# A decoder layer on one core: halved low parts of the keys, gate steps dealt by slot work, the down projection written token by token

## What is computed

```
a = rms_norm(h); projections of a: three mixers' q, k, v, and 3 x 1024 merge gates
A  sparse attention, 8 heads x 64: compressed keys (31 blocks), selected blocks, window of 256
B  differential attention, 4 heads: softmax(q1 k1) - lam softmax(q2 k2), values 128 wide, sub-norm
C  forgetting attention, 8 heads x 64, bias from a cumulated forget gate
merged = sum over mixers of sigmoid(gate) * (o @ w_br);  h = h + merged @ w_o
u, g = split(rms_norm(h) @ w_up);  h = h + (gelu(causal_conv3(u)) * g) @ w_down
```

## Time and profile before

| | us |
|---|---|
| median of 3 runs | 1049.41 |
| the profiled execution's own time | 1049.83 |
| its span in the trace | 1047.9 |
| TensorE busy | 1014.6 |
| VectorE busy | 576.9 |
| ScalarE busy | 413.0 |
| GpSimd busy | 80.8 |

### The profile page before, as it was taken

One profiled execution on the slowest core, in us unless ns is written; L12 is line 12 of the kernel. 1 busy time (PEld: TensorE's weight loads), 2 busy tenths in 40 slices (PEclk: granted clock), 3 DMA queues, 4 the chain that ended last, 5 costly groups with the idle time before them and its releaser, 6 DMA issues.

```text
span 1047.9 us, 13105 instructions
## 1 busy us (share of the span) xinstructions
PE 1014.6 (97%) x5133; PEld 850.4 (81%) x5133; DVE 576.9 (55%) x1056; ACT 413.0 (39%) x746; POOL 80.8 (8%) x66
## 2 busy tenths in 40 slices
PE   6899899999999999999899999999999999999998
PEld 5687789898887877888689888888888888888886
DVE  5645777773546678355655445465655656522123
ACT  4235445443446665424654433342322323221120
POOL 3200000000000000030000022011121111200000
PEclk9999899999999999999999999999999999999999
DMA  6512100102222211232211124222322323223222
GB/s 241 197 47 81 41 8 36 41 1 81 81 81 80 81 41 41 81 121 81 81 41 42 41 81 165 114 83 81 107 94 83 118 81 115 86 86 115 81 81 81
DMA packets 14653, 86.91 MB, mean 83 GB/s; under 512 B 1408, under 2 KB 3968, under 8 KB 5120
## 3 DMA queue, kind: packets, MB, share of 16 engines
q1 hardware_dynamic: 14592, 86.07, 23.1%
HBM read 83.96 MB, written 2.10 MB: 82 GB/s over the span
## 4 chain that ended last, share of the span: by engine, by line
PE 88%; DVE 7%; ACT 2%; issue 2%; DMA 1%; SPq 0%; DVEq 0%; ACTq 0%
PE ps L1280 20%; PE ps L1282 20%; PE ps L1281 20%; PE ps L1450 11%; PE ps L1436 5%; PE ps L1308 4%; PE ps L1422 2%; DVE k_ll L961 2%; PE ps L1423 2%; PE ps L1420 1%; DVE wl L855 1%; PE ps L1335 1%; PE ps L1413 1%; DVE nmx L1049 1%; DMA ident<-consts 1%
## 5 line engine op out<-in xcount | busy, mean ns | idle before, releaser
L855 DVE TENSOR_TENSOR wl<-raw,wh 128x512 fp32r<-128x512 f32 (+2 forms) x118 | 171.5, 1458 | 127.2 <-ACT wh L588 125.1
L588 ACT ACTIVATE wh<-raw 128x2048 fp32r<-128x2048 f32 (+1 forms) x58 | 109.4, 1886 | 155.9 <-PE ps L1282 138.3
L1280 PE MATMUL ps<-aT_h,wh 128*128 128x512 f32 (+1 forms) x376 | 146.7, 390 | 0.7 <-DVE aT_l L864 0.7
L1281 PE MATMUL ps<-aT_l,wh 128*128 128x512 f32 (+1 forms) x376 | 146.4, 389 | 0.0
L1282 PE MATMUL ps<-aT_h,wl 128*128 128x512 f32 (+1 forms) x376 | 146.4, 389 | 0.0
L737 ACT ACTIVATE prob<-ps,nmx 128x384 f32<-128x384 f32 (+3 forms) x128 | 66.7, 521 | 125.6 <-DVE nmx L1049 125.1
L1280 PE MATMUL ps<-wh,aT_h 128*128 128x512 f32 x256 | 102.4, 400 | 3.3 <-DVE smT L917 3.3
L1282 PE MATMUL ps<-wh,aT_l 128*128 128x512 f32 x256 | 101.1, 395 | 0.0
L1281 PE MATMUL ps<-wl,aT_h 128*128 128x512 f32 x256 | 100.9, 394 | 0.0
L1280 PEld LDWEIGHTS ps<-aT_h,wh 128*128 128x128 f32 (+1 forms) x376 | 70.0, 186 | 16.2 <-issue 0.9
L1282 PEld LDWEIGHTS ps<-aT_h,wl 128*128 128x128 f32 (+1 forms) x376 | 70.0, 186 | 15.3
(11 more groups left out here) (209 smaller groups left out, 1765.8 us busy)
## 6 DMA issues: line engine op xcount, KB each, us to landing
raw<-wblk SPq DMA_DIRECT2D x72, 1024.0 KB, 4.8
x<-x SPq DMA_DIRECT2D x4, 512.0 KB, 5.0
w_sb<-w SPq DMA_DIRECT2D x1, 2048.0 KB, 9.3
hid<-x SPq DMA_DIRECT2D x1, 2048.0 KB, 7.7
out<-outt SPq DMA_DIRECT2D x4, 512.0 KB, 3.1
stage<-consts SPq DMA_DIRECT2D x1, 1216.5 KB, 11.0
later<-consts SPq DMA_DIRECT2D x1, 448.0 KB, 12.0
par<-params SPq DMA_DIRECT2D x1, 204.5 KB, 7.8
```

The source lines that it names most:

```text
L588: nc.scalar.activation(wh[b % 2][:, 0:n], raw[b % RING][:, 0:n], ACT.Copy).then_inc(hi_ready, 4)
L855: ins = nc.vector.tensor_tensor(wl[b % RING][:, cols], raw[b % RING][:, cols], wh[b % 2][:, cols].bitcast(f32), ALU.subtract)
L1280: nc.tensor.matmul(dst, a_h, b_h, start=start, stop=False)
L1281: nc.tensor.matmul(dst, a_h, b_l, start=False, stop=False)
```

## The change

1. VectorE writes `k_ll` in DIFF and FOX in the head's own half only. GpSimd zeroes the other half once, after NSA's last scores, and TensorE waits for that (`k_zero`) ahead of DIFF's first unit. The product q_lo k_lo is left out.
2. ScalarE copies `small` to `smT`, ahead of its split of block `nq1`; VectorE no longer does.
3. NSA's first compressed scores, their norm, transposition and values stand ahead of unit 0, among 44 gate steps (40 before). The split of block `gate1` stands there too.
4. The other gate steps are dealt by an estimate of each slot's work (`slot_work`): the longer a slot keeps VectorE or ScalarE against TensorE, the more steps it gets. In DIFF most slots with an O get 0 to 2 and those with a C 5 to 13 (5 or 6 each before). In FOX slots get 9 falling to 1 (4 or 5 before). In NSA every second slot from 37 on gets none.
5. The down projection takes activations as the stationary operand and 512 weight columns as the moving one, so a bank holds 128 tokens by 512 output columns. `yT`, its copies and the 32 transposing matmuls go; VectorE adds bank and `hid` directly, and 8 DMAs of 256 KB send the result. `outt` lies at offset 0.

```diff
+def slot_work(m, events):
+    pe = dve = act = 0
+    for e in events:
+        if e[0] in ("S", "C", "A", "O"):
+            n = span(units_of(m)[e[1]])[1]
+        if e[0] == "S":
+            pe += 3 * (n * 2 // 5 + 20)
+            dve += n + 180
+            act += n * 4 // 5 + 420
+        elif e[0] == "C":
+            dve += 3 * n // 2 + 1000 if m == DIFF else 400
+        elif e[0] == "A":
+            pe += n * 5 // 6
+            if pv_index(m, e[1]) % 2:
+                act += n * 4 // 5 + 200
+            else:
+                dve += n + 150
+        elif e[0] == "O":
+            pe += n * 8 // 5
+            dve += 300
...
+    return pe, max(dve, act)
@@ attention_events
-        head += 8
-        put(-2, "SC", 0)
-        put(-1, "G", head, head + 8)
-        put(1, "CN", 0)
-        put(2, "TC", 0)
-        put(3, "OC", 0)
+        head += 20
...
-    for j in range(slots):
-        n = FILL - tail - head
-        put_fill(j, head + n * j // slots, head + n * (j + 1) // slots)
-        if j < U:
-            put(j, "S", j)
+    for j in range(U):
+        put(j, "S", j)
...
+    n = FILL - tail - head
+    work = [slot_work(m, at.get(j, [])) for j in range(slots)]
+    low, high = 0, 20000
+    while high - low > 1:
+        level = (low + high) // 2
+        if sum(max(0, max(level, 9 * o // 8) - p) for p, o in work) > n * 220:
+            high = level
+        else:
+            low = level
+    room = [max(0, max(high, 9 * o // 8) - p) for p, o in work]
+    done = 0
+    for j in range(slots):
+        f0 = head + n * done // sum(room)
+        done += room[j]
+        put_fill(j, f0, head + n * done // sum(room))
...
-        first += [("T", 0), ("G", HEAD_FILL[m], HEAD_FILL[m] + 8), ("T", 1)]
+        first = [("G", 0, 8), ("SC", 0), ("G", 8, 24), ("T", 0), ("CN", 0), ("G", 24, 32), ("T", 1), ("TC", 0), ("G", 32, 40), ("OC", 0), ("G", 40, head)]
+        for piece in range(4):
+            first[piece - 4:piece - 4] = [("W", BI[(m, "gate1")], piece), ("WL", BI[(m, "gate1")], piece)]
@@ scalar, NSA
                     split(BI[(m, "nq0")])
+                    full(act, ("P", m, "small", 0))
+                    b = place[("P", m, "small", 0)][0]
+                    nc.scalar.activation(smT[:, :], ps[b][0:32, :], ACT.Copy).then_inc(psum_free[b], 1)
                     split(BI[(m, "nq1")])
@@ vector
-                            lows = [k_ll[home, n, :], k_ll[other, n, :]]
+                            lows = [k_ll[home, n, :]]
...
             for d in range(KD):
-                if d % 2 == 1:
-                    full(dve, ("Y", d))
-                    b = place[("Y", d)][0]
-                    nc.vector.tensor_copy(yT[:, d, :], ps[b][:, :]).then_inc(psum_free[b], 1)
-                if d >= 2:
-                    finish(d - 2)
-            finish(KD - 2)
-            finish(KD - 1)
+                t, cols = d // 2, slice(d % 2 * S, d % 2 * S + S)
+                full(dve, ("Y", d))
+                nc.vector.tensor_tensor(outt[:, t, cols], bank(("Y", d))[:, :], hid[:, t, cols], ALU.add).then_inc(out_ready, 1)
@@ gpsimd
+            full(pool, ("S", NSA, len(units_of(NSA)) - 1))
+            nc.gpsimd.memset(k_ll[64:128, 0:8:2, :].bitcast(f32), 0.0)
+            nc.gpsimd.memset(k_ll[0:64, 1:8:2, :].bitcast(f32), 0.0).then_inc(k_zero, 1)
@@ tensor
+                            if m == DIFF:
+                                pe.wait_ge(k_zero, 1)
                         scores(j)
...
-                    cols = slice(d * P, (d + 1) * P)
+                    rows, cols = slice(d // 2 * P, d // 2 * P + P), slice(d % 2 * S, d % 2 * S + S)
                     for k in range(2):
-                        ins = passes(ps[d][:, :], h[:, k, cols], l[:, k, cols], acts[k][0], acts[k][1], first and k == 0, last and k == 1)
+                        f = 2 * n + k
+                        ins = passes(ps[d][:, :], actT_h[:, f, rows], actT_l[:, f, rows], h[:, k, cols], l[:, k, cols],
+                                     first and k == 0, last and k == 1)
                     if last:
                         done(("Y", d), ins)
-                        if d >= 2:
-                            finish(d - 2)
@@ sync
-            for n in range(4):
-                sp.wait_ge(out_ready, 2 * n + 2)
-                sp.dma_start(outv[:, :, n * 256:(n + 1) * 256], outt[:, :, n * 256:(n + 1) * 256]).then_inc(out_done, 16)
+            for d in range(KD):
+                t, cols = d // 2, slice(d % 2 * S, d % 2 * S + S)
+                sp.wait_ge(out_ready, d + 1)
+                sp.dma_start(outv[:, t, cols], outt[:, t, cols]).then_inc(out_done, 16)
```

More of the change, by code:

```diff
@@ L277, in build @@
         plan(("Y", d), d)
-    for d in range(KD):
-        plan(("YT", d), d)
     with ExitStack() as ctx:
@@ L832, in _ @@
                 split(B_DOWN + n)
-            for d in range(0, KD, 2):
-                full(act, ("Y", d))
-                b = place[("Y", d)][0]
-                nc.scalar.activation(yT[:, d, :], ps[b][:, :], ACT.Copy).then_inc(psum_free[b], 1)
         @block.vector
@@ L913, in post @@
                         ins.then_inc(cpe_ready, 1)
-                elif name == "small":
-                    full(dve, ("P", m, name, 0))
-                    b = place[("P", m, name, 0)][0]
-                    nc.vector.tensor_copy(smT[:, :], ps[b][0:32, :]).then_inc(psum_free[b], 1)
             def post_t(m, name, part=0):
@@ L1595, in _ @@
                         up_chunk(i, b, c)
-            def finish(d):
-                free(pe, ("Y", d))
-                transposes(("YT", d), [yT[:, d, t * P:(t + 1) * P] for t in range(TT)])
             def down(n):
@@ L1608, in down @@
                 h, l = [w[:, :].rearrange("p (k c) -> p k c", k=2) for w in (wh[blk % 2], wl[blk % RING])]
-                acts = [[t[:, 2 * n + k, :] for t in (actT_h, actT_l)] for k in range(2)]
                 for d in range(KD):
```

36 lines of the change are left out of this document (20 added, 16 removed).

## The result

| | before | change |
|---|---|---|
| median of 4 runs, us | 1049.38 (1049.29 to 1049.77) | 1042.7 (1041.7 to 1043.19) |
| the profiled execution's own time | 1049.83 | 1042.52 |
| its span | 1047.9 | 1040.7 |

The ratio is 0.9934, with a 95% interval of 0.9917 to 0.9952. So the change is faster, by 6.7 us where 24.3 were forecast. The time lies 10.7 us above the upper end of the range.

A forecast was written before the change was run, and what follows sets the result against it. The prediction took TensorE's own order, with its waits and half clock, to bound the kernel. Terms of -5.0, -5.6, -5.8, -2.3 and -5.6 sum to 24.3 us below the profiled 1049.83; with the median 0.4 lower, 1025.1 us, range 1021 to 1032.

The forecast's parts named there:

- Dealing the steps: Gate steps dealt by work: waits for `probT` in DIFF go, less new waits in slots without steps; -2.3 us.
- the 1.24 us: In DIFF, the time from a full transposition's start to the end of its copy, used to price slots without steps.
- The gain of 4.1 us: DIFF's four waits for VectorE's and two for ScalarE's `probT`, all expected to go under 8 to 13 steps.
- the dealing makes as many waits as it takes: Rival: DIFF gains nothing or loses, +4.9 instead of -2.3, NSA's thirteen stepless slots add 4; 1032 to 1036 us; chance 0.14.
- The first compressed scores: Start of NSA's units: the `pc` wait of 1.7 and half clock of 5.2 go, 1.3 of new waits come; -5.6 us.
- The wait of 0.7: NSA's wait behind SC 1, expected to stay because unit 5 needs the bank that SC 1 fills.
- Of the half clock I take all 5.2 us as gone: Start of NSA's units: seven steps ahead of SC 1, two before, were to remove the whole half-clock loss.
- the clock still falls: Rival: half clock remains at the start of NSA's units, two falls giving back 2 x 1.7 us, 1028.5 us; chance 0.2.
- The smT copy: Ahead of NSA: moving the copy to ScalarE removes a 3.3 us wait and 1.7 us of half clock; -5.0 us.
- The key lows: Keys of DIFF and FOX: two passes for a chunk bring the first score 2.9 us earlier in each; -5.8 us.
- Down projection: Last block and end: 2.7 us of transpositions go, and the tail shortens by 2.9 us to 3.7; -5.6 us.

The follow-up runs named there:

- e3: The change, but ScalarE takes the sub-norm's Ln and Exp right behind the square, so no Tanh comes between; 1030.94 us.
- e5: The kernel before, with a Tanh table load put ahead of the sub-norm's Ln in DIFF's first two chunks; 1055.66 us.
- e11: e8, with ScalarE loading Tanh's table again right behind `rstd` in DIFF's first three chunks; 1024.39 us.
- e7: e3, with each DIFF slot's share of gate steps half even and half by work; 1031.78 us.
- e6: e1, with compressed scores ahead of their slot's gate steps and six steps between T 1 and TC 0; 1025.43 us.
- e1: The change, but with gate steps dealt evenly again in DIFF alone; 1028.81 us.
- e4: The change, but with the event lists of the kernel before in all three mixers; 1031.97 us.
- e2: The change, but with gate steps dealt evenly in all three mixers; 1030.58 us.
- e12: The change with e6's order, e3's edit, at least even shares in DIFF's last four slots, and e11's early Tanh table load; 1024.73 us.
- e8: e7's dealing and edit together with e6's order at the compressed scores; 1027.6 us.

## Why the prediction was wrong

**Dealing the steps: the step that failed.** The sum took -2.3 us for it; measured was +12.7. It counted what steps give TensorE (cover) and what a copy takes (the 1.24 us), and nothing of what a step's end does to another engine: that a gate's 24th step puts a Tanh into ScalarE's list, whose tables depend on its neighbours. The four loads more were to be seen in the order of ScalarE's instructions ahead of the run; the prediction read that order for TensorE and VectorE only. e3 gives this part 9.9 us. e5 shows that such loads alone, without dealing, make 6.6. The last 2.7 us are, as far as shown, again a load, that of the third chunk's Tanh just ahead of the tail: moving the loads (e11) took them away in e7's dealing. In the change's own dealing that was not run, but e3, which has it, shows the same load (at 397.32) and the same 2.19 us of VectorE behind it. There the prediction did see a wait, "0.9 us at unit 29, which has no scores between", and took the copy of probabilities alone for its cause. It was 1.83 us, with the clock falling behind it, for the copy stands in VectorE's order behind the combination of unit 31, which waits for its own scores' max and exponential. The gain of 4.1 us was not there either: the waits for `probT` are 5.0 us in sum in the change and 4.8 in e3. With the loads moved, half a dealing by work is 1.0 us ahead of even dealing (e11: 100.6, e6: 101.6), not 2.3, and as e6 kept its loads where they cost it as much, dealing itself may be worth nothing.

The recorded rival *the dealing makes as many waits as it takes* had the right place in part but another mechanism, slots without steps. e7 gives these slots steps, and the stretch wins nothing. Its size, +4.9, was too small too. Its second half, waits in the thirteen slots of the sparse mixer, did not come: the list has none there.

**The first compressed scores: -5.6, measured -3.5.** The wait at TC 0 was worked out as 1.0 and was 1.36, for another reason: the sum let the norm end it, but `pc` was ready at 100.70 + 0.43 = 101.1 us. TC 0 began at 101.93, when the first of T 1's lows (VectorE, from 101.04) had freed the bank that both use. The wait of 0.7 stayed, as said. What failed was "Of the half clock I take all 5.2 us as gone": of 10.2 us at half clock there 6.8 stayed. Seven steps ahead of SC 1 did not prevent it. That is the rival *the clock still falls*, with its price of 3.4 us for two falls a little high. The same program in this stretch ran with 6.8 us of half clock in e1 and with none in e3, and NSA took 169.9 and 167.2 us: 2.7 us, not 3.4, for e3 has a wait of 0.40 for `probT` at 121.96 that e1 has not. The kernel before and e4 have the same events there; e4 has 6.8 us of half clock less and is 1.6 us faster, because waits that the slow clock had covered come out (0.78 us for `probT` at 118 us). Against e6, which has no such new wait, e1's half clock comes out at its full 3.4.

The rival cites the Trainium skill, "TensorE: Matmul & The Clock Gate" (Part 4: PE-mode transpose), by which transpositions are no work for the gate. By that rule T 0, T 1 and TC 0 are no cover, and six real steps between them, as in e6, should help; no fall came there. But e6 takes two waits away as well, and e3 and e1 differ in this with one and the same program. So the runs neither show nor refute it.

**The smT copy: -5.0.** The wait is gone, the clock is 1.0, and the stretch is 6.4 us shorter. As the profiled run of the change began 0.7 us later, some of it is made good by inputs that come at their own time: e1 to e6 begin like before, and this stretch is 5.2 to 5.7 us shorter in e1, e2 and e3.

**The key lows: -5.8, measured -5.4** (2.65 and 2.74). The waits of 0.6 were 0.7 to 0.9, two in each mixer: ahead of a key transposition and ahead of the first score. **Down projection: -5.6, measured -5.4:** 2.3 for the transpositions where 2.7 were taken, 3.1 for the tail, whose new length is 3.54 us against 3.7.

**The sum.** 6.4 + 3.5 + 5.4 + 5.4 = 20.7 us were won, against 22.0 forecast for these parts; less 0.7 for the later start and 12.7 and 0.1 in DIFF and FOX this leaves 7.2, the difference of the spans. The forecast of a gain held; the number fails by the dealing. e6, without dealing in DIFF and with cover at TC 0, comes to 1025.43 us, the forecast's number. It is no support for it: in e6 NSA gives 8.3 us, not 5.6, and DIFF nothing.

**A version better than both:** e11, at 0.9762 of the time before [0.9748, 0.9775], 18 us below the change. e12 and e6 are the same within their intervals.

What stays open: why the same program has its clock fall at 114 us in one run and not in another. In NSA the change, e1, e3 and e7 are one program with the same waits of 1.36 and 0.7 us. Behind the wait at 114.60 us (e1) and 114.70 (the change) the clock fell for 6.8 us; behind the same wait at 114.66 (e7) and 115.05 (e3) it did not, and e7 has a fall of 3.4 us at 144 us instead. So the place in the span doesn't decide it. Executions of one kernel differ too: e1's four lie in two pairs, 1027.8 us at a mean clock of 0.999 and 1029.8 at 0.997. Also open are even dealing with the early load, the early load in the change's own dealing, and what short cover at the tail costs by itself; it is known only as the wait of 1.55 us.

## What to carry to other kernels

When filler work is dealt anew, follow what its last step sets off on every other engine, not only how much TensorE has to do: here a Tanh landed between a table's preload and its use and cost four times what the dealing was to give. Read the order of the table loads on ScalarE after each such move, keep a preload and its uses in one uninterrupted piece, and load the table back at once, where ScalarE has slack, and not at the next use, where somebody waits.

## What was not expected of the hardware

- **Ln and Exp load apart when their common set isn't preloaded.** With the preload, one load of 1.28 us serves both (before: 363.93, then 366.21 and 366.53 without a load). Once Tanh has been between, L646 and L647 each load, 2.56 us. The kernel before shows it too, at the norm of DIFF's first projection, where nothing preloads: L600 at 263.80 and L601 at 265.42 load 1.28 us each. The Trainium skill, "ScalarE: Activation LUTs" (Table sets: the hidden batching unit), says that ln followed by exp is one load. In these traces that holds only behind the preload of the set. The same page (What ACT_TABLE_LOAD costs) gives about 1283 ns for a load, as the rows do, and further some 1380 ns of drain; here Ln starts 0.01 us after the end of the load (356.78 + 1.28, 358.07), so no drain is seen.
- **A load on an engine off the path can cost more than its 1.28 us.** Four more loads, 5.1 us of ScalarE, an engine busy 40% of the span, made 9.9 us of TensorE's time (e3), for VectorE stood 4.25 us idle until `rstd` with scores and copies queued behind, and the clock fell after it. Three loads of the same length, only moved, gave 4.2 us in the traces and 3.2 in the medians (e8 and e11).
- **Half clock can cost less than half its length near waits:** 2.7 us (e1 and e3) and 1.6 us (before and e4) for 6.8 us of it, where full speed brought out waits that the slow clock had covered. Between e1 and e6 the same 6.8 us cost the full 3.4.
